# A two-layer encoder on one core: a Mamba scan with one decay block a head, and down projections that begin with two units in one pass

## The chip, the cores and the metric

The kernel runs on one core of a Trainium2 chip. The metric is the device time of one execution in microseconds (us). The median of three runs of the kernel before is 2797.76 us (2797.67 to 2798.13).

## The reference

Batch 1, 256 tokens, width 2048, two layers, all in float32. Layer 0 is a gated short convolution mixer and an MLP, layer 1 a bidirectional Mamba-2 mixer (64 heads of 64 channels in 8 groups, state 128, chunks of 128 tokens) and an MLP of the same form; each of the four sublayers has an adaLN modulation of its own from the condition vector.

```
for each sublayer:  shift, scale, gate = split(silu(c) @ ada_w + ada_b)
                    h = rms_norm(x, g) * (1 + scale) + shift
                    x = x + gate * sublayer(h)
MLP:    square(relu(h @ w1)) @ w2                       (2048 -> 8192 -> 2048)
conv:   b, c, v = split(h @ w_in);  (b * dwconv3(c * v)) @ w_out
Mamba:  z, x, B, C, dt_raw = split(h @ w_in); x, B, C = silu(dwconv3(.) + bias)
        dt = softplus(dt_raw + dt_bias), one forward and one backward for each head
        per direction: cum = running sum of dt * a;  y[t] = sum over s of
              (C[t] . B[s]) * exp(cum[t] - cum[s]) * dt[s] * x[s],   s <= t (backward: s >= t)
        y = y_fwd + y_bwd + d * x;  u = group_rms_norm(y * silu(z)) * g;  u @ w_out
```

## The kernel before, in words

Activations lie as channels x tokens (16 blocks of 128 channels, 256 tokens). Each float32 product is made of three: the weights are split into a high half `wh` (fp32r) and a rest `wl`, the activations into a high and a low part that lie side by side in `hcat` (input of a layer) or `hid` (between its two products). One **unit** makes 128 output channels: two halves of weights, 16 blocks of the contraction, for each block one matmul of `wh` against 512 columns and one of `wl` against 256 (L918, L921), into one of the two PSUM banks `psm`. For a unit `v`, in each engine's order:

- SP loads the raw weights of half after half (512 KB, four buffers) and, where the schedule has one, a 1 MB tile of modulation weights into `adat` (two buffers).
- ACT (`step`, `unit`) makes the high half of half 2v+4 (L674), copies bank v to `ta` (L679), and makes the high half 2v+5.
- DVE (`step`) makes the low half 2v+4 (L1121), adds the two parts of the bank into `tt` or `pad` (L1153, L1200, L1279), makes the low half 2v+5, does what the unit needs besides, and reduces a modulation tile where there is one (L1134).
- POOL makes low parts of activations (L558, L592) and adds to the residual `x` (L548).

A unit of PE waits until unit v-2 has been added (`at_least(pe, summed, u - 1)`), since it shares that unit's bank. `pair` (L928 on) is a second form: two units at once, block by block, into both banks; it waits for `summed` of u, that is also for the unit just before it. Before, it is used for the first units behind each norm, for the dt projection and for the first two output units of the Mamba mixer (`src == "chunk 0"`). All other down projections (`gated`) start with single units, whose first one waits block by block for the blocks of `hid` that its predecessor, an up projection or conv unit, is still making.

The order is written out in `walk`: conv (24 pairs of triples), its output (16 units), MLP 0 in four quarters of 16 up and 16 down units, dt, groups 0 to 4, the first output units of the Mamba mixer (over the channels of groups 0 to 3), groups 5 to 7, the late output slabs (`late_outs`, half a unit each), MLP 1 in four quarters.

A **group** of the Mamba mixer is ten units, called slots 0 to 9: B, C, four blocks of x, four of z. The scan of group g-1 runs between the units of group g, that of group 7 between the late slabs. Its steps by slot, before:

- Slot 0: PE makes the scores (L1014) and transposes x to tokens (L1020). ACT copies two blocks of scores (L793, L794) and the transposed x (L798). POOL multiplies x by the dt of each direction, from `dgrp` (two operations of 1024 columns, L582). DVE masks the scores into `gcat` (L1333).
- The running sums lie in DRAM; SP loads them, broadcast, into `em[1..4]` (four pieces of two heads each). `em[1]` lies in `normt`, `em[2]` and `em[3]` in `dec`, `em[4]` in the second buffer of `adat`, which is why SP holds modulation tiles back there (`resume`).
- `segments` (DVE, L1375, four operations of 128 columns) and `decays` (ACT, L785, four exponentials of 256 columns) for pieces 1 to 4; piece 1's segments come at the end of the group before, the other pieces' in slots 0 to 2, the decays in slots 0 to 3.
- `masked` in slots 1 to 4 (DVE, L1303, L1305, L1309): products of decays and scores into 3 x 128 columns for each direction.
- Slots 3 to 6: PE makes two heads each (L1034), for each head three products for either block of tokens, so 12 in a slot. A float32 product shows as two records.
- Slot 6: ACT copies y out of PSUM (L802). Slot 7: PE transposes it back (L1043), DVE adds the skip term and multiplies by z (L1318, L1323). Slots 8 and 9: the group norm (L805, L586, L1050, L808, L1340, L1344), then the high and low parts for the output product (L818, L592).
- `columns_of` (DVE, L1354, L1357), at the end of each group: the group's 8 columns of dt and sums are copied out of `dtS` and `ncS`, and the gaps between blocks made.

`dt_late` makes dt and the sums in group 0; `DT_ALL` is the count of its DVE steps after which the sums may be used.

In a slot DVE's order is `scan_piece`, low half, `scan_mid` (here `masked`), silu of the unit before, addition, low half, taps, `scan_late` (here `segments`); ACT's is `scan_piece`, high half, copy, high half, centre tap, tanh, `scan_late` (here `decays`).

## Time and profile before

| | before |
|---|---|
| median of 3 runs | 2797.76 us |
| profiled execution | 2797.92 us |
| its span (first to last instruction) | 2796.2 us |
| mean granted TensorE clock | 0.982 |
| PE busy | 2601.4 us, 93% |
| DVE busy | 2140.2 us, 77% |
| ACT busy | 1354.1 us, 48% |
| POOL busy | 781.6 us, 28% |
| read from HBM | 675.58 MB, 242 GB/s over the span |

Busy shares are means over stages that differ. The Mamba part lies between 1236 and 2050 us, the conv layer and MLP 0 ahead of it, MLP 1 behind it. A row of the waits says which engine and instruction waited for which; a row of the timeline has its start, its duration (of all merged instructions, if x is over 1), and in brackets the idle time ahead of it with what ended it. Matmuls overlap, so durations of several don't add up: the distance from start to start is what counts.

### The profile page before, as it was taken

The page shows a single profiled execution, that of the slowest core. Times are in us where ns is not written, and L with a number is a line of the kernel's source. Part 1 is how long each engine was busy: PE and PEld are TensorE (multiplying, and loading weights), DVE is VectorE, ACT ScalarE, POOL GpSimd, SP SyncE. Part 2 cuts the span into 40 slices and gives each one's busy share as a digit, 9 for nine tenths or more (in the row PEclk, how much of TensorE's full clock was granted, in tenths as well). Part 3 has the DMA queues.
Part 4 walks back from the last instruction along what each step waited for, and adds up shares of the span by engine and source line. Part 5 has one row for each costly group of instructions (what it writes and reads, how often), then busy time and mean ns, then how long its engine had stood idle before and what let it go on. Part 6 is the DMA issues. An engine that isn't in the chain of part 4 may idle for free. (4 is left out here: it accounts for less than half of the span.)

```text
span 2796.2 us, 45031 instructions
## 1 busy us (share of the span) xinstructions
PE 2601.4 (93%) x14956; PEld 2269.0 (81%) x14956; DVE 2140.2 (77%) x2597; ACT 1354.1 (48%) x2038; POOL 781.6 (28%) x714
## 2 busy tenths in 40 slices
PE   0399999999999999999999899999989999999998
PEld 0288888888888888878888788888878888888887
DVE  6988889886978879986777787778799555555554
ACT  2244444544444444465555544556454444444454
POOL 3522225442434434530111031111345111111123
PEclk9899999999999999999999999999999999999999
DMA  8888889686878879945554485555559555555554
GB/s 331 306 321 318 316 330 363 239 315 229 331 287 314 316 280 324 358 168 196 166 166 166 158 311 207 167 166 165 204 215 338 192 188 188 188 188 188 189 188 142
DMA packets 171670, 679.62 MB, mean 243 GB/s; under 512 B 18672, under 2 KB 35312, under 8 KB 146704
## 3 DMA queue, kind: packets, MB, share of 16 engines
q1 hardware_dynamic: 171488, 677.75, 68.6%
q8 instruction: 79, 1.29, 0.2%
q14 instruction: 55, 0.45, 0.0%
q0 software_dynamic: 48, 0.13, 0.0%
HBM read 675.58 MB, written 2.23 MB: 242 GB/s over the span
## 5 line engine op out<-in xcount | busy, mean ns | idle before, releaser
L1121 DVE TENSOR_TENSOR wl<-raw,wh 128x1024 fp32r<-128x1024 f32 x862 | 1130.0, 1311 | 461.6 <-ACT wh L674 459.7
L918 PE MATMUL psm<-hcat,wh 128*128 128x512 f32 x3984 | 1270.0, 400 | 16.0 <-DVE pad L1279 10.8
L674 ACT ACTIVATE wh<-raw 128x1024 fp32r<-128x1024 f32 x866 | 911.0, 1052 | 215.8 <-PE psm L921 141.4
L921 PEld LDWEIGHTS psm<-hcat,wl 128*128 128x128 f32 x3984 | 755.4, 190 | 179.6
L918 PE MATMUL psm<-hid,wh 128*128 128x512 f32 x2528 | 797.7, 397 | 10.2 <-POOL hid L558 5.7
L921 PE MATMUL psm<-hcat,wl 128*128 128x256 f32 x3984 | 788.7, 280 | 0.0
L918 PEld LDWEIGHTS psm<-hcat,wh 128*128 128x128 f32 x3984 | 613.7, 191 | 19.3 <-issue 13.2
L921 PEld LDWEIGHTS psm<-hid,wl 128*128 128x128 f32 x2528 | 476.4, 188 | 112.5
L921 PE MATMUL psm<-hid,wl 128*128 128x256 f32 x2528 | 497.7, 278 | 0.0
L1134 DVE CUSTOM_DVE_ANT_0 adat<-adat,cond 128x2048 f32<-128x2048 f32 x176 | 427.0, 2426 | 21.1 <-DMA adat<-in_ada 13.8
L918 PEld LDWEIGHTS psm<-hid,wh 128*128 128x128 f32 x2528 | 386.4, 189 | 12.0 <-POOL hid L558 7.0
L558 POOL TENSOR_TENSOR hid<-tt,hid 128x256 f32 (+1 forms) x128 | 176.3, 1377 | 481.5 <-ACT hid L742 481.5
L548 POOL TENSOR_TENSOR x<-x,tt 128x256 f32 (+1 forms) x154 | 198.5, 1289 | 400.7 <-DVE tt L1200 400.7
L510 POOL COPY modc<-modt 128x1 f32 (+1 forms) x192 | 175.4, 919 | 233.4 <-DVE modt L1134 233.4
L679 ACT ACTIVATE ta<-psm 128x256 f32<-128x256 f32 x257 | 96.7, 376 | 182.9 <-PE psm L921 176.7
L742 ACT ACTIVATE hid<-tt 128x256 f32 (+1 forms) x128 | 53.5, 418 | 266.4 <-DVE tt L1222 266.4
L679 ACT ACTIVATE ta<-psm,mods 128x256 f32<-128x256 f32 x160 | 75.5, 472 | 215.3 <-PE psm L921 209.8
L1200 DVE SCALAR_TENSOR_TENSOR tt<-psm,mods,ta 128x256 f32<-128x256 f32 x160 | 76.6, 479 | 108.5 <-ACT ta L679 108.3
L586 POOL TENSOR_TENSOR zs<-zs 128x512 f32<-128x512 f32 x8 | 10.4, 1294 | 402.0 <-ACT zs L805 402.0
L940 PE MATMUL psm<-hcat,wh 128*128 128x512 f32 x128 | 49.1, 469 | 78.5 <-POOL wl L656 55.8
L683 ACT ACTIVATE normt<-x 128x256 f32<-128x256 f32 (+1 forms) x80 | 33.3, 417 | 141.8 <-POOL x L548 100.1
L1153 DVE TENSOR_TENSOR tt<-ta,psm 128x256 f32<-128x256 f32 x177 | 73.1, 413 | 23.6 <-ACT ta L679 23.6
(174 smaller groups left out, 1684.7 us busy)
## 6 DMA issues: line engine op xcount, KB each, us to landing
raw<-in_w SPq DMA_DIRECT2D x866, 512.0 KB, 4.2
adat<-in_ada SPq DMA_DIRECT2D x176, 1024.0 KB, 6.4
xs<-in_ada SPq DMA_DIRECT2D x8, 1024.0 KB, 6.7
zs<-in_ada SPq DMA_DIRECT2D x8, 1024.0 KB, 6.2
dec<-running_sums SPq DMA_DIRECT2D x32, 256.0 KB, 5.3
normt<-running_sums SPq DMA_DIRECT2D x16, 256.0 KB, 4.7
adat<-running_sums SPq DMA_DIRECT2D x16, 256.0 KB, 5.3
x<-in_xT SPq DMA_DIRECT2D x1, 2048.0 KB, 17.1
```

Source lines behind the costliest of these rows:

```text
L510: pool.tensor_copy(modc[:, bass.ds(a.v, 1)], modt[:, a % 2:a % 2 + 1]).then_inc(mod_copied, 1)
L548: pool.tensor_tensor(x[:, nn.v, :], x[:, nn.v, :], tt[:, v % 2, :], ALU.add).then_inc(stored, 1)
L558: pool.tensor_tensor(hid[:, jj.v, T:2 * T], tt[:, v % 2, :], hid[:, jj.v, 0:T].bitcast(F32), ALU.subtract).then_inc(stored, 1)
L674: act.activation(wh[:, h % 4, :], raw[:, h % 4, :], ACT.Copy).then_inc(hi_done, 1)
L679: act.activation(ta[:, v % 2, :], psm[v % 2][:, 0:T], ACT.Copy, scale=scale).then_inc(copied, 1)
L742: act.activation(hid[:, jj.v, 0:T], tt[:, v % 2, :], ACT.Copy).then_inc(relu_hi, 1)
L918: pe.matmul(bank[:, :], wh[:, h % 4, (k + i) * P:(k + i + 1) * P], src[:, kb + i, :], start=(kb + i == 0), stop=(kb + i == KB - 1), skip_g ...
L921: mm = pe.matmul(bank[:, T:2 * T], wl[:, h % 4, (k + i) * P:(k + i + 1) * P], src[:, kb + i, 0:T], start=False, stop=(kb + i == KB - 1), s ...
L1121: dve.tensor_tensor(wl[:, h % 4, :], raw[:, h % 4, :], wh[:, h % 4, :].bitcast(F32), ALU.subtract).then_inc(lo_done, 1)
L1134: dve.tensor_tensor_reduce(t, t, cond[:, :], 1.0, 0.0, ALU.mult, ALU.add, modt[:, a % 2:a % 2 + 1]).then_inc(ada_done, 1)
L1153: return dve.tensor_tensor(tt[:, v % 2, :], ta[:, v % 2, :], psm[v % 2][:, T:2 * T], ALU.add)
L1200: return dve.scalar_tensor_tensor(out=tt[:, v % 2, :], in0=psm[v % 2][:, T:2 * T], scalar=gcol, in1=ta[:, v % 2, :], op0=ALU.mult, op1=ALU ...
```

## The change

The scan: one decay block per head and per block of tokens. Inside a block both directions go into one 128 x 128 matrix (the dt of each direction is multiplied in on ACT and DVE, in `decays` and `masked`), so that a head needs two products instead of six. What crosses from one block of tokens to the other is made by two products 128 x 512 for all eight heads of a group, from x weighted by `far_in` (POOL), into `psr[1]` and `psr[0]`, and scaled by `far_out` when y is gathered, which DVE now does in place of ACT's copy. The columns `far_in`, `far_out` and the gaps are made once for all heads in `dt_late`, and `columns_of` is gone. The buffers of pieces 1 and 4 move (`hv`, a third `dec`), so that modulation tiles are no longer held back.

The down projections: `gated` on PE begins with `pair` wherever its first unit follows a change of source, in nine more places (the conv's output, four quarters of MLP 0, four of MLP 1).

```diff
-DT_AV, DT_TOK, DT_CUM, DT_ALL = 11, 13, 14, 15
+DT_AV, DT_TOK, DT_CUM, DT_FAR, DT_ALL = 11, 13, 15, 22, 24
...
-        em = [None, normt[:, :].rearrange("p (k t) -> p k t", k=4), dec[:, 0], dec[:, 1]]
-        em.append(adat[:, 1, 0:6 * T].rearrange("p (k t) -> p k t", k=4))
+        em = [None, hv, dec[:, 0], dec[:, 1], dec[:, 2]]
+        columns = normt[:, 4 * T:6 * T].rearrange("p (n d h) -> p n d h", n=4, d=2)
+        far_in, far_out, gapS, midS = (columns[:, i] for i in range(4))
...
@@ SP, load_sums @@
                 at_least(sp, y_head, g * HG + HG)
-                if piece == 4:
-                    at_least(sp, ada_done, ADA_LATE if g.c >= GA - 1 else ADA_OUT0)
...
@@ POOL, scan_piece, slot 0 @@
                     at_least(pool, xt_copied, g * 2 + 2)
-                    at_least(pool, grp_in, g * 2 + 2)
-                    for d in (1, 0):
-                        if d == 0:
-                            at_least(pool, xd_ready, g * 2 + 1)
-                        src, dst = (xd[:, i, :, :].rearrange("p c (h e) -> p c h e", e=HD) for i in (0, d))
-                        pool.tensor_tensor(dst, src, dgrp[:, :, d, :].unsqueeze(3).to_broadcast([P, 2, HG, HD]),
+                    pool.wait_ge(dt_dve, DT_ALL)
+                    for d in range(2):
+                        src, dst = (xd[:, i, d, :].rearrange("p (h e) -> p h e", e=HD) for i in (0, 1))
+                        pool.tensor_tensor(dst, src, far_in[:, d, heads(g)].unsqueeze(2).to_broadcast([P, HG, HD]),
                                            ALU.mult).then_inc(xd_ready, 1)
...
@@ ACT @@
+            def dt_far():
+                act.wait_ge(dt_dve, DT_FAR)
+                act.activation(far_in, far_in, ACT.Exp).then_inc(dt_act, 1)
+                act.activation(far_out, far_out, ACT.Exp, scale=-1.0).then_inc(dt_act, 1)
...
             def decays(g, piece):
                 at_least(act, seg_done, g * 4 + piece)
-                for d in range(2):
+                act.wait_ge(dt_dve, DT_ALL)
+                at_least(act, g_ready, g * 4 + 4)
+                for c in range(2):
+                    here = slice(c * P, (c + 1) * P)
                     for i in range(2):
-                        row, h = em[piece][:, 2 * d + i, 0:T], 2 * (piece - 1) + i
-                        ins = act.activation(row, row, ACT.Exp, bias=ngrp[:, d, d, h:h + 1])
+                        own, other = em[piece][:, 2 * c + i, here], em[piece][:, 2 * (1 - c) + i, here]
+                        h = g.c * HG + 2 * (piece - 1) + i
+                        act.activation(own, own, ACT.Exp, bias=ncS[:, c, c, h:h + 1])
+                        ins = act.activation(other, lower[c], ACT.Copy, scale=dtS[:, c, 1, h:h + 1])
...
-                if s == 6:
-                    at_least(act, y_head, g * HG + 2 * HG)
-                    for ch in range(2):
-                        act.activation(ytok[:, ch, :], psy[ch][:, :], ACT.Copy).then_inc(y_tok, 1)
...
@@ PE, gated @@
-                both = first and src == "chunk 0"
-                if both:
+                if first:
                     pair(u, ready, hid)
-                for s in range(2 if both else 0, 4):
-                    unit(u + s, hid, ready if first and s == 0 else None)
+                for s in range(2 if first else 0, 4):
+                    unit(u + s, hid)
...
@@ PE, scan_piece @@
                 if 3 <= s <= 6:
+                    if s == 3:
+                        at_least(pe, g_copied, g * 2 + 2)
+                        at_least(pe, g_ready, g * 4 + 4)
+                        at_least(pe, xd_ready, g * 2 + 2)
+                        pe.matmul(psr[1][:, :], gf[:, P:T], xd[:, 1, 0, :], start=True, stop=True, skip_group_check=True)
+                        pe.matmul(psr[0][:, :], gb[:, 0:P], xd[:, 1, 1, :], start=True, stop=True, skip_group_check=True)
                     for h in (2 * (s - 3), 2 * (s - 3) + 1):
...
-                        for ch, terms in ((0, ((mf, 0, 0, 0), (mb, 2 * P, 1, 0), (mb, 0, 1, 1))),
-                                          (1, ((mf, P, 0, 0), (mf, 2 * P, 0, 1), (mb, P, 1, 1)))):
-                            for i, (m, at, d, sc) in enumerate(terms):
-                                mm = pe.matmul(psy[ch][:, cols], m[:, at:at + P], xd[:, d, sc, cols],
-                                               start=(i == 0), stop=(i == 2), skip_group_check=True)
+                        for ch in range(2):
+                            mm = pe.matmul(psy[ch][:, cols], em[s - 2][:, 2 * ch + h % 2, ch * P:(ch + 1) * P],
+                                           xd[:, 0, ch, cols], start=True, stop=True, skip_group_check=True)
...
@@ DVE, dt_late, slot 9 @@
+                    dve.wait_ge(dt_dve, DT_CUM + 1)
+                    for d in range(2):
+                        own(dve.tensor_tensor(gapS[:, d, :], ncS[:, d, 1 - d, :], ncS[:, d, d, :], ALU.subtract))
+                        own(dve.tensor_tensor(far_in[:, d, :], ncS[:, d, d, :], midS[:, d, :], ALU.add))
+                        own(dve.tensor_tensor(far_out[:, d, :], ncS[:, 1 - d, d, :], midS[:, d, :], ALU.add))
+                    dve.wait_ge(dt_act, 6)
+                    for d in range(2):
+                        own(dve.tensor_tensor(far_in[:, d, :], far_in[:, d, :], dtS[:, d, d, :], ALU.mult))
...
@@ DVE, masked @@
-                dve.tensor_tensor(e[:, 0:2, T:3 * P], e[:, 2:4, P:T],
-                                  gf[:, T:3 * P].unsqueeze(1).to_broadcast([P, 2, P]), ALU.mult)
-                dve.tensor_tensor(e[:, 2:4, T:3 * P], e[:, 0:2, 0:P],
-                                  gb[:, T:3 * P].unsqueeze(1).to_broadcast([P, 2, P]), ALU.mult).then_inc(far_done, 1)
-                at_least(dve, far_done, g * 4 + piece)
-                e4 = e[:, :, 0:T].rearrange("p (d i) t -> p d i t", d=2)
-                dve.tensor_tensor(e4, e4, gcat[:, :, 0:T].unsqueeze(2).to_broadcast([P, 2, 2, T]), ALU.mult)\
-                    .then_inc(em_ready, 1)
+                for c in range(2):
+                    for i in range(2):
+                        h = g.c * HG + 2 * (piece - 1) + i
+                        other = e[:, 2 * (1 - c) + i, c * P:(c + 1) * P]
+                        ins = dve.scalar_tensor_tensor(out=other, in0=upper[c], scalar=dtS[:, c, 0, h:h + 1], in1=other,
+                                                       op0=ALU.mult, op1=ALU.add)
+                ins.then_inc(sel_done, 1)
+                at_least(dve, sel_done, g * 4 + piece)
+                for c in range(2):
+                    own, other = (e[:, 2 * k:2 * k + 2, c * P:(c + 1) * P] for k in (c, 1 - c))
+                    ins = dve.tensor_tensor(own, own, other, ALU.mult)
+                ins.then_inc(em_ready, 1)
...
@@ DVE, scan_piece, ahead of the slot's low half @@
+                if s == 6:
+                    at_least(dve, y_head, g * HG + 2 * HG)
+                    for ch in range(2):
+                        dve.tensor_tensor(ytok[:, ch, :].rearrange("p (h e) -> p h e", e=HD),
+                                          psr[ch][:, :].rearrange("p (h e) -> p h e", e=HD),
+                                          far_out[:, 1 - ch, heads(g)].unsqueeze(2).to_broadcast([P, HG, HD]),
+                                          ALU.mult).then_inc(y_far, 1)
+                    at_least(dve, y_far, g * 2 + 2)
+                    for ch in range(2):
+                        dve.tensor_tensor(ytok[:, ch, :], ytok[:, ch, :], psy[ch][:, :], ALU.add).then_inc(y_tok, 1)
...
-            def columns_of(g):
...
@@ DVE, group @@
                 silu(g, u + (GU - 1), GU - 1)
-                columns_of(g)
                 segments(g, 1)
```

## Rows read from the trace of the kernel before

**Rows 1.** The waits of PE from 1236 to 2050 us: total, times, longest.

```profile
PE psm L918 <- DVE pad L1279: 10.8, 6, 1.9
...
PE psr L1082 <- issue: 4.6, 1, 4.6
```

**Rows 2.** Windows: length, busy of PE, PEld, DVE, ACT, POOL, PEclk, DMA share, GB/s.

```profile
500.00:1216.00 716.00, 713.26 (x4080) 621.17 (x4079) 601.63 (x622) 340.31 (x476) 295.82 (x227) 1.00 0.82 300
...
2162.00:2165.30 3.30, 3.24 (x10) 2.76 (x11) 1.84 (x4) 2.39 (x3) 0.14 (x2) 0.51 0.09 35
```

**Rows 3.** The timeline of DVE in slots 0 and 1 of a group: start, duration.

```profile
1460.82 0.42 DVE L1279 TENSOR_TENSOR pad<-ta,psm 128x256 f32<-128x256 f32 x1
...
1462.30 0.48 DVE L1285 SCALAR_TENSOR_TENSOR acc<-pad,parg,acc 128x256 f32<-128x256 f32 x1
...
1466.32 1.23 DVE L1121 TENSOR_TENSOR wl<-raw,wh 128x1024 fp32r<-128x1024 f32 x1 [1.98 <-ACT wh L674]
1467.46 0.42 DVE L1303 TENSOR_TENSOR normt<-normt,gcat 128x256 f32<-128x256 f32 x1
...
1469.39 0.42 DVE L1392 SCALAR_TENSOR_TENSOR bT<-th,acc 128x256 f32<-128x256 f32 x1
1469.73 0.41 DVE L1279 TENSOR_TENSOR pad<-ta,psm 128x256 f32<-128x256 f32 x1
```

**Rows 4.** The timeline of ACT in the same slots.

```profile
1463.65 1.69 ACT L785 ACTIVATE normt<-normt,ngrp 128x256 f32<-128x256 f32 x4
1465.25 1.04 ACT L674 ACTIVATE wh<-raw 128x1024 fp32r<-128x1024 f32 x1
```

**Rows 5.** The timeline of PE: the first two heads, the transposes of slot 7.

```profile
1469.62 2.87 PE L1034 MATMUL psy<-xd,normt 128*128 128x64 f32 x24 [0.86 <-DVE normt L1309]
...
1505.75 1.09 PE L1043 MATMUL psr<-ident,xd 128*128 128x128 f32 x8 [0.98 <-ACT xd L802]
```

**Rows 6.** Groups by line and shape: busy us, mean ns of one, idle before.

```profile
L1014 PE MATMUL psr<-cT,bT 128*128 128x256 f32 x32 | 8.2, 379 | 0.0
...
L793 ACT ACTIVATE gcat<-psr 128x128 f32<-128x128 f32 x8 | 2.1, 258 | 0.0
```

**Rows 7.** The timeline of POOL and DVE at the end of a group.

```profile
1451.75 2.44 POOL L592 TENSOR_TENSOR hid<-xs,hid 128x1024 fp32r<-128x1024 f32 x1 [12.48 <-ACT hid L818]
...
1454.30 3.89 POOL L582 TENSOR_TENSOR xd<-xd,dgrp 128x1024 f32<-128x1024 f32 x2
...
1529.59 2.44 POOL L592 TENSOR_TENSOR hid<-xs,hid 128x1024 fp32r<-128x1024 f32 x1 [12.49 <-ACT hid L818]
...
1451.95 2.42 DVE L1357 TENSOR_TENSOR gap<-ngrp 128x8 f32<-128x8 f32 x2
1454.48 4.38 DVE L1375 SCALAR_TENSOR_TENSOR normt<-normt,gap 128x128 f32<-128x128 f32 x4
```

**Rows 8.** The timeline of DVE at the end of group 0.

```profile
1301.92 1.14 DVE L1375 SCALAR_TENSOR_TENSOR normt<-normt,gap 128x128 f32<-128x128 f32 x4 [4.92 <-DMA normt<-running_sums]
```

**Rows 9.** The timeline of PE and DVE where down projections begin, and behind the existing pass.

```profile
2336.87 0.63 PE L918 MATMUL psm<-hid,wh 128*128 128x512 f32 x2
...
2337.60 0.42 DVE L1153 TENSOR_TENSOR tt<-ta,psm 128x256 f32<-128x256 f32 x1 [0.30 <-ACT ta L679]
...
948.88 0.63 PE L918 MATMUL psm<-hid,wh 128*128 128x512 f32 x2
...
950.57 0.41 DVE L1153 TENSOR_TENSOR tt<-ta,psm 128x256 f32<-128x256 f32 x1
...
2152.19 0.68 PE L918 MATMUL psm<-hid,wh 128*128 128x512 f32 x2
...
2157.35 0.41 DVE L1153 TENSOR_TENSOR tt<-ta,psm 128x256 f32<-128x256 f32 x1
...
2162.06 0.80 PE L918 MATMUL psm<-hid,wh 128*128 128x512 f32 x1 [4.54 <-POOL hid L558]
...
1619.91 0.47 PE L918 MATMUL psm<-hid,wh 128*128 128x512 f32 x1 [1.17 <-DVE tt L1200]
```

More of the change, by code:

```diff
@@ L135, in first_unit, with heads @@
     return g * GU + U_GA
+def heads(g):
+    return slice(g.c * HG, g.c * HG + HG)
 def blocks(g):
@@ L203, in build @@
         ncS = sb("ncS", [P, 2, 2, HEADS])
-        dec = sb("dec", [P, 2, 4, 3 * P])
+        dec = sb("dec", [P, 3, 4, T])
         bT = sb("bT", [P, T])
@@ L388, in load_half, with load_ada @@
                 sp.dma_start(raw[:, h % 4, :], w[h.v]).then_inc(raw_in[h % 4], 16)
-            def load_ada(a, resumed=False):
-                if not a.terms and (a.c >= ADA or a.c - ADA_OUT0 in (0, 1) and not resumed
-                                    or a.c - ADA_LATE in (0, 1) and not resumed):
+            def load_ada(a):
+                if not a.terms and a.c >= ADA:
                     return
@@ L473, in norm @@
                 sp.wait_ge(out_done, 64)
-            def resume(a, g):
-                at_least(sp, y_head, g * HG)
-                for k in range(2):
-                    load_ada(a + k, True)
             walk(sp, lambda u, j, ada_at, a, f: steps(u, 6, ada_at, a),
@@ L484, in _ @@
                  lambda: steps(At(U_DT), 1, (), None),
-                 group, late_outs, norm, resume=resume)
+                 group, late_outs, norm)
         @block.gpsimd
@@ L827, in group @@
                         dt_log()
+                    elif s == 9:
+                        dt_far()
             def late_outs(a):
@@ L996, in dt_late @@
                                   start=False, stop=False, skip_group_check=True)
-                        mm = pe.matmul(psr[2][rows, far * P:(far + 1) * P], avS[:, far, rows], up[:, :],
-                                       start=False, stop=True, skip_group_check=True)
+                        pe.matmul(psr[2][rows, far * P:(far + 1) * P], avS[:, far, rows], up[:, :],
+                                  start=False, stop=True, skip_group_check=True)
+                    for near, rows in ((0, f), (1, b)):
+                        mm = pe.matmul(psr[3][:, rows], ones[:, :], avS[:, near, rows], start=True, stop=True,
+                                       skip_group_check=True)
                     mm.then_inc(dt_pe, 1)
@@ L1268, in dt_late @@
                     own(dve.tensor_copy(hv[:, 0, :], psr[2][:, 0:T]))
+                    own(dve.tensor_copy(midS.rearrange("p d h -> p (d h)"), psr[3][:, 0:P]))
                 if s == 9:
@@ L1367, in segments @@
                 at_least(dve, cb_in[s - 1], g * 32 + 32)
[L1368 to L1369 removed]
+                dve.wait_ge(dt_dve, DT_ALL)
                 for c in range(2):
@@ L1372, in segments @@
                     for i in range(2):
-                        h = 2 * (s - 1) + i
+                        h = g.c * HG + 2 * (s - 1) + i
                         own, other = em[s][:, 2 * c + i, here], em[s][:, 2 * (1 - c) + i, here]
-                        ins = dve.scalar_tensor_tensor(out=own, in0=other, scalar=gap[:, c, h:h + 1], in1=own,
+                        ins = dve.scalar_tensor_tensor(out=own, in0=other, scalar=gapS[:, c, h:h + 1], in1=own,
                                                        op0=ALU.add, op1=ALU.min)
```

29 lines of the change are left out of this document (4 added, 25 removed).

## The prediction

> **What bounds the kernel now.** First read who TensorE (PE) waits for. A projection, conv or MLP unit is 32 matmuls, at 716 us for 4080 of them (127.5 units) 5.6 us, and nearly everywhere the next follows at once [rows 2]. Between 1236 and 2050 us (the Mamba part) the wait that comes again in the groups is for the DVE addition that empties a unit's bank, six times and 10.8 us [rows 1]. So less PE work pays only where others are not later still, and the second look goes to what DVE and ACT do in a group.
>
> In a slot of a group (one unit) DVE runs, in this order: a low half, `masked`, a silu, the addition into `pad`, a low half, two taps, `segments`. ACT runs tanh, `decays`, a high half. These lean on each other in a ring: addition to first tap 1.48 us, first tap to `decays` (over tanh) 1.35, `decays` to high half 1.60, high half to DVE's low half 1.07, low half to `masked` 1.14, `masked` to silu 1.93, silu to addition 0.34 [rows 3, 4]. That is 8.91 us, just the distance of the two additions, 1460.82 and 1469.73 [rows 3]. Four such turns follow each other in a group (slots 0 to 4), 35.6 us. In those slots PE needs the unit and two heads (24 records in 2.87 us, 0.11 each beside the tail), 8.4 us, and waits for `masked` ahead of them [rows 5]. **The ring is slower than PE already.** The other slots are PE's. POOL's first step of a group comes again after 77.84 us [rows 7].
>
> **The scan, step by step.**
> (a) PE: 24 records become 8 for two heads, 16 x 0.11 = 1.76 us less in each of four slots, 7.0 a group. Two products 512 wide come; one 256 wide is 8.2/16 = 0.51 us [rows 6], so about 0.9 each, 1.8 a group. Net 5.2 us a group on PE, but in slots where it waits. What counts is the ring.
> (b) ACT: `decays` issues 8 instructions of 128 columns for 4 of 256. Bounds for one: 0.40 us (1.60/4, width costing nothing), and 0.155, a plain 128-wide copy's 0.258 less the 0.1 by which neighbours overlap (a `decays` instruction among four, 1.69 in all, overlaps so too) [rows 4, 6]. They read bias or scale from a column as the 0.40 ones do, and half the width should save about 0.11, so I take 0.29: 2.3 us, +0.7 a turn, between -0.4 and +1.6.
> (c) DVE `masked`: four 128-wide instructions with a column scalar, like `segments` (1.14 for four [rows 8]), then two of 256 elements at 0.34 (silu to addition [rows 3]): 1.82 for 1.93, -0.1. A turn becomes 9.5 us, four +2.4; by the bounds -1.9 to +6.0.
> (d) `columns_of` goes, and POOL multiplies 2x512 columns instead of 2x1024. Now DVE's two tiny subtractions take 2.42 us while POOL makes a low part of 2.44, and four `segments` instructions take 4.38 (elsewhere 1.14) and end at 1458.86, 0.67 after POOL's 3.89 us of products [rows 7, 8]. The products halve, so DVE is free 1.9 to 2.5 us earlier; I take 2.1.
> The Trainium skill, SBUF — State Buffer, section "SBUF: two separate sides", says that a DVE operation with two SBUF inputs and a GpSimd operation that reads SBUF exclude each other for a whole instruction, and the later one blocks. By that rule, the trace agrees; if they shared bandwidth instead, the dropped subtractions would count in full and the sum would be some 5 us lower.
> (e) y leaves PSUM by DVE instead of ACT, in four operations of 512 columns. The 256-wide addition issues in 0.34, the 1024-wide low half in 1.14 [rows 3], so 0.60 each, with 0.25 for the dependence and the tail 2.65 us. DVE comes to it after slot 5's taps: from the fourth turn's addition A a turn without `decays` and `masked` is 5.4, low half and taps 2.5, so A+7.9, done A+10.55. PE starts the transposes at 1505.75, which is A+9.3 (A is 1460.82+35.62), after a wait of 0.98 for ACT's copy [rows 5]. So +1.25 us, and all of slots 7 to 9 stands behind it. ACT wins its copies' time back and has no use for it.
> In five groups the first addition waits for POOL: -2.1 + 2.4 + 1.25 = +1.5 each, 7.5 us. In two (the first scanned, and the first behind the output units) PE's own queue was as late, and nothing is won at (d): +3.5 each, 7 us.
> (f) The decay columns are made once, at the end of group 0: six small subtractions or additions, two exponentials, two products, ahead of the count for which SP waits before it issues the loads of sums. DVE waits 4.92 us for their landing already [rows 8]. It all moves back by 2.2 us (ten at 0.15 to 0.2, a crossing to ACT and back). SP's raw loads queue behind; four buffers cover them.
> (g) Group 7 is scanned among the late output slabs, where PE waits 4.6 us once [rows 1]. (d) takes 2.1 of that; four head slots lose 1.76 each less 1.8 for the wide products, but a slab then waits for a DVE sum behind the slower ring. I take 7 us less (2 to 9).
> (h) PE will idle about 4 us before the transposes (its unit ends at A+6.3, y is there at A+10.55), and 2 to 3 us before heads. After a wait of 4.54 us for `hid` [rows 9] the granted clock was 0.51 over the next 3.3 us [rows 2], the 1.2 GHz level, so 1.65 us of work was lost. Before slot 7 this counts in full, in slots 1 to 5 the slack covers it. Some 0.7 us a group: 5 (0 to 12).
> (i) The loads of modulation tiles are no longer held back for the scan's buffer, and the copies of columns go. Nothing waits for either but (d); 0.
> Scan: 7.5 + 7 + 2.2 + 5 - 7 = +15 us.
>
> **The down projections.** Nine places (the conv's output, four quarters of each MLP) now begin with two units in one pass. It needs both banks, so PE must wait until the last up unit is copied by ACT and added by DVE, where now the first down unit starts at once. In three quarters of the last MLP it starts as at 2336.87, and the addition ends at 2338.02 [rows 9]: 1.17 us new, three times 3.5. In three of the first MLP's, behind a slow low half, as from 948.88 to 950.98 [rows 9]: 2.1, three times 6.3. By the same reading 3.5 at its first quarter, 4.4 at the conv's output, and at the last MLP's first quarter, where DVE is behind with modulation tiles, 2152.19 to 2157.76 [rows 9], 5.6. Sum 23.3 us. Behind the pass the next unit waits for copy and addition again, as behind the one existing pass over `hid`: 1.17 us idle [rows 9], 1.34 start to start above the usual step, nine times 12.1. What goes: the pass comes to the last block 5 us later, so the present waits for it vanish, 4.7 (idle 4.54 [rows 9]), 3.5 and 1.3 in three places, 9.5 us. The other six wait for no block now. Net 23.3 + 12.1 - 9.5 = +25.9. Half clock after the longer waits 3 us (0 to 8). DVE idles in the pass and has two units' additions and tiles behind it, 2 us (0 to 5). **+31 us.** A free bank would cover the entry, and there is none.
>
> **Sum.** 15 + 31 = +46 on the profiled execution's 2797.92 us (span 2796.2 and 1.7 around it; the median of the runs is 2797.76, the same): 2844 us.
>
> **Rivals.**
> 1. The ring shrinks below PE. If `decays` ran in ACT's idle time, off the ring, a turn would be 7.3 us, four 29.2 for 35.6; with (d) and (e) -7.3 a group, -51 in seven: 2797.9 + 31 - 51 - 7 = 2771, faster. It decides where a turn falls below 7.9 us (28 turns must return 45 us). For it: ACT has idle time in each turn. Against: its program has `decays` behind tanh and ahead of the high half that DVE waits for. 7%.
> 2. The entries of the passes cost nothing, because DVE comes to the addition sooner than now: 2844 - 23 - 3 = 2818. Against: nothing ahead of the boundary changes. 6%.
> 3. ACT's narrow instructions cost 0.155: -1.9 - 2.1 + 1.25 = -2.7 in five groups, -0.6 in two, +2.2, -7 to -9, no half clock: scan -20, 2797.9 + 26 to 31 - 20, 2804 to 2809. 9%; the lower half of it is within reach of no change.
> 4. Half clock throughout: each head slot with 2 to 3 us of idle runs at 1.2 GHz, a unit takes up to 11 us for 5.6, and PE leads again by some 2 us in each of 28 slots: 2844 - 5 + 56 = 2895. Against: waits of 1.9 us [rows 1] leave the slots behind them mostly at full clock. 3%. The Trainium skill, TensorE: Matmul & The Clock Gate, section "HAM oscillation — how this bites in real kernels", has such a case, a kernel whose idle gaps between bursts bring the lower clock back each time.
> My case as summed: 75%.
>
> **Numbers.** 2844 us. Range 2809 to 2867: the low end is (b) near its lower bound, the high end (b) at 0.40 (+3.6 in seven groups, 25, less 2 for slack). A difference of 0.2% (5.6 us) is about what a measurement of this kernel can tell from none. Faster 0.09, within 0.04, slower 0.87.
>
> **What would show it.** In the profile after: additions into `pad` 9.5 us apart in slots 0 to 4 (above 9 supports (b), below 8.5 refutes it); PE gaps before heads of 2 to 3 us and before the transposes of about 4, both ended by DVE; nine passes with a wait for a DVE `tt` ahead (1.2, 2.1, or 3.5 to 5.6 us) and one of 1.2 behind; no wait for `hid` left; a middle group's period near 80 us. I am wrong if that is below 76, or if PE enters the passes without a wait.

## The result, and the profile after

| | before | after |
|---|---|---|
| median | 2797.95 us | 2887.43 us |
| lowest and highest of 4 runs | 2797.67 to 2800.89 | 2886.08 to 2888.44 |
| span of the profiled execution | 2796.2 us | 2885.3 us |
| mean granted TensorE clock | 0.982 | 0.970 |

Ratio 1.0317, 95% interval 1.0299 to 1.0335: slower by 89.5 us, where 46 were forecast, and above the range. The direction was right; the size was not, so the question is what the other 43 us are.

First the waits of TensorE in the profile after, 1290 to 2126 us, the Mamba part as in [rows 1] (columns: who waited for whom, us in total, times, the longest):

```profile
engine line waited for: us in total, times, longest us
PE psy L1035 <- DVE dec L1323: 42.5, 18, 2.8
PE psr L1044 <- DVE xd L1361: 40.3, 8, 6.5
PE psy L1035 <- DVE normt L1323: 8.2, 7, 1.3
```

The wait for `pad`, first in [rows 1], is gone. Two others have come: for the masked decays ahead of the heads (2.8 us and less), which the prediction named, and for y ahead of the transposes: 40.3 us in 8, up to 6.5, where "about 4" stood. Next the additions into `pad` and `masked` ahead of them on DVE, after (start, duration, instruction), to hold against [rows 3]:

```profile
1505.07 0.42 DVE L1289 TENSOR_TENSOR pad<-ta,psm 128x256 f32<-128x256 f32 x1
...
1512.47 1.13 DVE L1317 SCALAR_TENSOR_TENSOR normt<-gcat,dtS,normt 128x128 f32<-128x128 f32 x4
1513.63 0.76 DVE L1323 TENSOR_TENSOR normt<-normt 128x256 f32<-128x256 f32 x2
...
1514.65 0.41 DVE L1289 TENSOR_TENSOR pad<-ta,psm 128x256 f32<-128x256 f32 x1
...
1524.21 0.41 DVE L1289 TENSOR_TENSOR pad<-ta,psm 128x256 f32<-128x256 f32 x1
...
1533.76 0.41 DVE L1289 TENSOR_TENSOR pad<-ta,psm 128x256 f32<-128x256 f32 x1
```

They are 9.56 us apart, forecast 9.5. But the group has a period of 83.2 us, where the forecast had "near 80" (77.8 before). On ACT the eight exponentials and copies of `decays` stand 0.29 us apart (three of them):

```profile
1507.90 0.39 ACT L785 ACTIVATE normt<-normt,ncS 128x128 f32<-128x128 f32 x1
1508.20 0.39 ACT L786 ACTIVATE normt<-gcat,dtS 128x128 f32<-128x128 f32 x1
1508.49 0.39 ACT L785 ACTIVATE normt<-normt,ncS 128x128 f32<-128x128 f32 x1
```

So the ring did what was said, and the loss lies behind it. Then the end of the scan of the same group, DVE:

```profile
1550.16 0.48 DVE L1295 SCALAR_TENSOR_TENSOR acc<-pad,parg,acc 128x256 f32<-128x256 f32 x1
1550.68 0.48 DVE L1298 SCALAR_TENSOR_TENSOR acc<-pad,parg,acc 128x256 f32<-128x256 f32 x1
1552.59 1.23 DVE L1122 TENSOR_TENSOR wl<-raw,wh 128x1024 fp32r<-128x1024 f32 x1 [1.43 <-ACT wh L665]
1553.74 1.28 DVE L1355 TENSOR_TENSOR xd<-psr,normt 128x512 f32<-128x512 f32 x2
1555.05 1.28 DVE L1361 TENSOR_TENSOR xd<-xd,psy 128x512 f32<-128x512 f32 x2
```

y (L1355, L1361; `ytok` lies in `xd`) doesn't follow the taps (L1298), as the prediction has it, but the low half behind them (L1122), which waits 1.43 us for ACT's high half. TensorE then:

```profile
1556.39 1.97 PE L1044 MATMUL psr<-ident,xd 128*128 128x128 f32 x8 [6.54 <-DVE xd L1361]
1558.01 1.20 PE L917 MATMUL psm<-hcat,wh 128*128 128x512 f32 x2
```

With the fourth turn's addition A at 1543.32, that is A+13.1 for a forecast of A+10.55. And eight transposes take 1.97 us for 1.09 [rows 5], the two products behind them 1.20 for 0.62: half clock. The first MLP's first pass has it as well, the last MLP's second has not (rows of the windows: stretch, length, busy time of PE, PEld, DVE, ACT, POOL, granted clock, DMA share, GB/s):

```profile
599.40:602.80 3.40, 3.34 (x12) 2.89 (x13) 1.51 (x3) 0.42 (x1) 0.73 (x1) 0.59 1.03 372
...
2417.30:2428.70 11.40, 11.35 (x64) 9.79 (x64) 2.79 (x3) 1.89 (x3) 0.74 (x1) 1.00 0.43 138
1556.40:1559.70 3.30, 3.30 (x14) 3.06 (x15) 3.04 (x7) 0.42 (x1) 0.00 (x0) 0.58 0.20 30
```

The granted clock 0.59 over a stretch that ends at full speed is the 1.2 GHz level. That pass was entered after 3.35 us of idleness, the one at full clock after 1.12, and both are left after 1.58 to 1.60:

```profile
599.46 0.72 PE L939 MATMUL psm<-hid,wh 128*128 128x512 f32 x2 [3.35 <-DVE wl L1122]
...
614.00 0.70 PE L917 MATMUL psm<-hid,wh 128*128 128x512 f32 x2 [1.58 <-DVE tt L1201]
```

```profile
2417.35 0.72 PE L939 MATMUL psm<-hid,wh 128*128 128x512 f32 x2 [1.12 <-DVE tt L1154]
...
2428.36 0.40 PE L943 MATMUL psm<-hid,wl 128*128 128x256 f32 x2
2430.36 0.73 PE L917 MATMUL psm<-hid,wh 128*128 128x512 f32 x2 [1.60 <-DVE tt L1201]
```

**Where the time went.** Both executions have the same products of weights in nearly the same order, and the starts of the same ones cut both into stages. A down projection is counted from the last product ahead of it to its own last one. What each stage takes more than before, in us, for the profiled execution of the changed kernel and of experiments below ("first": the first group that scans; "behind out": the group behind the output units; "rest": start, norms, group 0, output units). Where a kernel has no edit, such a sum can still differ by 3 us: before_decays_early changes nothing in the down projections.

| | down projections (9) | first | behind out | other 5 groups | late slabs | rest | all |
|---|---|---|---|---|---|---|---|
| predicted | 31 | 6.4 | 4.2 | 11.0 | -7 | 0 | 46 |
| predicted, less its half clock | 28 | 5.7 | 3.5 | 7.5 | -7 | 0 | 38 |
| **after** | 42.2 | 9.6 | 7.5 | 30.0 | -3.0 | 2.9 | 89.2 |
| scan_alone | 0.3 | 9.5 | 7.5 | 30.2 | -3.0 | 1.7 | 46.2 |
| pass_alone | 42.5 | -0.2 | 0.0 | 0.2 | -0.6 | 1.9 | 43.8 |
| y_ahead | 40.7 | 7.6 | 4.7 | 19.9 | -7.0 | 1.5 | 67.5 |
| warm_pass | 31.6 | 10.3 | 7.8 | 30.7 | -3.0 | 3.2 | 80.7 |
| warm_y | 40.8 | 7.9 | 5.1 | 20.6 | -4.6 | 2.5 | 72.4 |
| y_ahead_warm | 31.6 | 6.9 | 2.4 | 9.4 | -7.0 | 3.8 | 47.2 |
| decays_early | 40.5 | 1.9 | 0.0 | -9.2 | -4.5 | 3.2 | 31.9 |
| before_decays_early | 3.1 | -4.8 | -3.6 | -21.9 | -0.3 | -2.2 | -29.7 |
| best_no_pass | 0.8 | 0.1 | -3.8 | -22.4 | -6.9 | -0.2 | -32.4 |
| best_y_warm | 1.4 | -3.7 | -6.6 | -38.3 | -6.3 | 1.1 | -52.3 |

### The profile page after: what moved, and what is told of

It is laid out like the page before. It is cut to its first block and busy times, and to the rows that moved or that the text cites. A ratio compares the mean times of both kernels' runs of the same rounds, so it can differ in the third digit from the quotient of the medians.

```text
span 2885.3 us, 44320 instructions
## 1 busy us (share of the span) xinstructions
PE 2595.8 (90%) x14480; PEld 2244.3 (78%) x14480; DVE 2149.6 (75%) x2702; ACT 1366.6 (47%) x2152; POOL 770.0 (27%) x714
## 5 line engine op out<-in xcount | busy, mean ns | idle before, releaser
L1122 DVE TENSOR_TENSOR wl<-raw,wh 128x1024 fp32r<-128x1024 f32 x862 | 1135.3, 1318 | 512.9 <-ACT wh L665 510.8
L917 PE MATMUL psm<-hid,wh 128*128 128x512 f32 x2240 | 706.6, 397 | 15.2 <-DVE tt L1201 15.0
L917 PEld LDWEIGHTS psm<-hcat,wh 128*128 128x128 f32 x3984 | 620.1, 193 | 10.1 <-DVE wl L1122 6.5
L920 PEld LDWEIGHTS psm<-hid,wl 128*128 128x128 f32 x2240 | 420.8, 188 | 99.4
L920 PE MATMUL psm<-hid,wl 128*128 128x256 f32 x2240 | 440.3, 278 | 0.0
L917 PEld LDWEIGHTS psm<-hid,wh 128*128 128x128 f32 x2240 | 340.9, 189 | 19.0 <-issue 10.0
L939 PE MATMUL psm<-hid,wh 128*128 128x512 f32 x320 | 110.4, 429 | 26.3 <-DVE wl L1122 16.2
L577 POOL TENSOR_TENSOR zs<-zs 128x512 f32<-128x512 f32 x8 | 10.4, 1303 | 453.5 <-ACT zs L802 453.5
```

Of the source, the lines that this page charges most:

```text
L917: pe.matmul(bank[:, :], wh[:, h % 4, (k + i) * P:(k + i + 1) * P], src[:, kb + i, :], start=(kb + i == 0), stop=(kb + i == KB - 1), skip_g ...
L920: mm = pe.matmul(bank[:, T:2 * T], wl[:, h % 4, (k + i) * P:(k + i + 1) * P], src[:, kb + i, 0:T], start=False, stop=(kb + i == KB - 1), s ...
L939: pe.matmul(bank[:, :], wh[:, h % 4, k * P:(k + 1) * P], src[:, kb, :], start=(kb == 0), stop=(kb == KB - 1), skip_group_check=True)
L1122: dve.tensor_tensor(wl[:, h % 4, :], raw[:, h % 4, :], wh[:, h % 4, :].bitcast(F32), ALU.subtract).then_inc(lo_done, 1)
```

## The experiments

Twelve kernels ran. Eleven have the median of four or five executions, with the kernel before timed beside them (2798.2 to 2799.0 us); peel_all has a single execution. "Less" is the difference to the changed kernel's 2887.4, where nothing else is said.

**scan_alone and pass_alone.** The change in its two parts. The first has the change without the new passes, the second the new passes alone:

```diff
 # PE, gated
-                if first:
+                both = first and src == "chunk 0"
+                if both:
                     pair(u, ready, hid)
-                for s in range(2 if first else 0, 4):
-                    unit(u + s, hid)
+                for s in range(2 if both else 0, 4):
+                    unit(u + s, hid, ready if first and s == 0 else None)
```

> The kernel after with the down projections begun by single units again, so the scan's edit alone. Theory: the two parts add up, and the scan carries +44 to +48 us (47 us more in the eight stretches that hold a group's scan, 3 less in the late slabs): 2840 to 2846 us. A group of the middle keeps its period of 83 to 84 us. Rival: the two parts lean on each other (half clock or DVE's backlog carried over from the passes), then the scan alone is below +35 us.

> The kernel before with its down projections begun by two units in one pass in the nine places, so this edit alone. Theory: +40 to +44 us, 2838 to 2842 us, with 3.3 us in each quarter of the last MLP and 5.7 in the first MLP's. My prediction had +31. Rival: the passes alone cost the predicted 31 us, and the rest comes from the scan's edit (buffers moved, modulation tiles loaded sooner).

Measured 2844.38 us (ratio 1.0163, interval 1.0146 to 1.0180) and 2843.26 (1.0161, 1.0144 to 1.0178), +46 and +45. The second is 1.3 us above what was expected. They add up to the change's 89.5 within 2 us, and the stages of either are those of the whole: the parts hardly touch each other. Both are dearer than forecast, the scan by 31 us, the passes by 14.

**y_ahead.** Is it the place of y? The four DVE operations go from `scan_mid` (behind the low half) to `scan_piece` (ahead of it):

```diff
             def scan_piece(g, s):
                 par2 = g % 2
+                if s == 6:
+                    at_least(dve, y_head, g * HG + 2 * HG)
...
+                        dve.tensor_tensor(ytok[:, ch, :], ytok[:, ch, :], psy[ch][:, :], ALU.add).then_inc(y_tok, 1)
                 if s == 7:
```

> The kernel after with DVE's gathering of y moved ahead of slot 6's low half, which is where my prediction had it; in the change it stands behind that low half, which waits for ACT. Theory: PE's wait before the transposes falls by 2.6 us in each of seven groups and the half clock behind it partly goes: 18 to 26 us less than the kernel after, 2861 to 2869 us. Rival: the low half is then late by the 2.6 us of the gathering and PE waits for it instead, 0 to 5 us less.

Measured 2862.86 us (1.0230, 1.0213 to 1.0247): 24.6 less. The wait ahead of the transposes is now 3.87 us in all seven groups:

```profile
1547.96 1.97 PE L1044 MATMUL psr<-ident,xd 128*128 128x128 f32 x8 [3.87 <-DVE xd L1337]
```

With A at 1537.55 that is A+10.4, for the forecast's A+10.55. The late slabs win the 7 us that (g) gave them. The stages give 21.7 us, not 24.6, because the profiled execution was 2.5 us slower than the median: 14.9 in the groups, 4.0 in the late slabs.

**decays_early.** Is it the ring that sets the slots? `decays` is issued behind ACT's second high half of the slot instead of ahead of the first one:

```diff
 # ACT, unit
                 copy(v, 1.0 if conv_unit else 0.5)
                 hi(v * 2 + 5)
+                if early:
+                    early()
 # ACT, group
+                    early = (lambda s=s: decays(g - 1, s + 1)) if scanning and s <= 3 else None
+                    unit(g, u + s, s, scanning, early)
-                    unit(g, u + s, s, scanning)
-                    if scanning:
+                    if scanning and s > 3:
                         scan_late(g - 1, s)
```

> The kernel after with the decays of slots 0 to 3 issued by ACT before the centre tap, in the time in which it waits for DVE's addition, instead of behind tanh (in the groups; the late slabs are left). Theory (a ring of DVE and ACT sets slots 0 to 4): a turn falls from 9.56 by the 2.3 us of decays to 7.2 to 7.6, and with four turns in seven groups 50 to 65 us go: 2822 to 2837 us. Rival (PE sets these slots, through its half clock): additions stay 9 us and more apart or PE fills the time, less than 15 us go.

Measured 2830.24 us (1.0115, 1.0098 to 1.0132), 57 less. The additions:

```profile
1503.16 0.41 DVE L1294 TENSOR_TENSOR pad<-ta,psm 128x256 f32<-128x256 f32 x1
...
1507.06 1.23 DVE L1127 TENSOR_TENSOR wl<-raw,wh 128x1024 fp32r<-128x1024 f32 x1 [0.39 <-ACT wh L665]
...
1510.38 0.41 DVE L1294 TENSOR_TENSOR pad<-ta,psm 128x256 f32<-128x256 f32 x1
```

7.22 us apart, where rival 1 had 7.3. Four turns are 9.4 us shorter; a group is 7.5 to 7.8 shorter, since TensorE's waits for y grow from 40.3 us to 47.5.

**before_decays_early.** The same move in the kernel before.

> The kernel before with only its decays moved behind ACT's high half. Ours: a turn's ring falls from 8.91 to 7.3 us there as well, below TensorE's own 8.4 us with 24 records a head pair, so four turns return 4 x 0.5 = 2 us a group, 14 in seven, and somewhat more where the first addition is late: 2775 to 2786 us. So the move is worth less there than in the changed kernel (57 us), because TensorE is the next bound. Rival, the move is worth the same in both: 2741 us. Rival, TensorE was the bound all along: 2796 to 2799.

Measured 2768.84 us (0.9895, 0.9879 to 0.9912), 29.6 less: twice what I expected, half of the other. TensorE is the next bound, as said: its heads come 8.27 us after each other. But a middle group gains 4.2 to 4.7 us, not 2. In the one that starts at 1370 us slot 2 gives 1.1, each of slots 3 to 5 0.6, and slot 6 1.2, where TensorE's wait for y ahead of the transposes, 0.98 us before [rows 5], is gone.

The trace also shows what I had not seen: the kernel before has half clock in six of its seven groups that scan. In four it follows the 1.9 us wait for `pad` [rows 1] (behind the one that ends at 1461.39 the granted clock is 0.61 over 3.3 us), in two a wait of 2.1 or 2.4 us for `masked`. With `decays` early it is left in three groups. It explains little of the gain: two groups with as much of it as before (1.7 us of work lost) gain 4.2 us, two that lose all 3.4 us of it gain 4.6 and 4.7.

**warm_pass and warm_y.** Is the longer work behind an idle stretch half clock, and what does it cost? TensorE multiplies the identity into an idle bank ahead of the wait; each such product takes 0.23 to 0.25 us. (Both kernels already do so ahead of the sums of three norms, in `keep_warm`.)

```diff
-            def pair(u, ready, src=hcat):
+            def pair(u, ready, src=hcat, warm=0):
+                for _ in range(warm):
+                    pe.matmul(psy[1][:, 0:P], ident[:, :], ident[:, :], start=True, stop=True,
+                              skip_group_check=True)
+                    warm = (16, 7, 0, 20 if isinstance(src, At) and src.c == U_MLP1 and not src.terms else 0)[layer]
+                    pair(u, ready, hid, warm)
-                    pair(u, ready, hid)
 # PE, scan_piece, warm_y
                 if s == 7:
+                    if warm:
+                        for _ in range(18):
+                            pe.matmul(psr[3][:, 0:P], ident[:, :], ident[:, :], start=True, stop=True,
+                                      skip_group_check=True)
                     at_least(pe, y_tok, g * 2 + 4)
```

> The changed kernel with products of the identity into an unused bank (16, 7 and 20 of them, about 0.23 us each) on TensorE ahead of the waits of six passes: the conv's output, the first MLP's four, the last MLP's first. If the 1.5 us (2.1 at the last MLP's first) by which these passes are longer than the other three (12.97 for 11.4 us) is the half clock after the idle entry, they end 1.2 to 1.8 us earlier each: 2877 to 2881 us. If the longer passes are something else (waits for weights or blocks inside), 2886 to 2889.

> The changed kernel with 18 such products (4.2 us) on TensorE ahead of its wait for y in slot 7 of seven groups. The transposes (1.97 us for 8) and the first blocks of the unit behind them run at half clock after 5.0 to 6.5 us of idleness. If that costs in full, as slot 7 is TensorE's, 1.0 to 1.7 us a group come back: 2876 to 2881 us. If the half clock there is covered by a later wait: 2885 to 2888.

Measured 2878.24 us (1.0284, 1.0267 to 1.0302), 9.2 less, and 2870.98 (1.0260, 1.0243 to 1.0277), 16.5 less. In warm_y:

```profile
1545.52 4.18 PE L1041 MATMUL psr<-ident 128*128 128x128 f32 x36
1552.20 1.09 PE L1048 MATMUL psr<-ident,xd 128*128 128x128 f32 x8 [2.51 <-DVE xd L1365]
1553.05 0.71 PE L917 MATMUL psm<-hcat,wh 128*128 128x512 f32 x2
```

```profile
1552.20:1555.50 3.30, 3.29 (x22) 2.99 (x23) 3.30 (x7) 0.42 (x1) 0.00 (x0) 1.00 0.19 55
```

22 records in the 3.3 us behind the wait, for 14 above, and clock 1.00 after 2.51 us of idleness. In warm_pass the first pass of the first MLP takes 11.4 us for 12.97. So longer useless work made the kernel faster, and by more than I had put even on a whole scan's half clock.

**y_ahead_warm.** Both corrections at once, with 12 products ahead of the transposes.

> The changed kernel with the two steps that the prediction had wrong put right: y gathered ahead of slot 6's low half, as the prediction placed it, and products of the identity on TensorE ahead of the long waits (12 ahead of the transposes of y in seven groups, 16, 7 and 20 ahead of six passes). In y_ahead units 7 and 8 of a group and the transposes take 2.7 us more than at full clock (13.19 for 11.40, 1.97 for 1.09); the passes gave 9.2 us back. If placement and half clock are all that the prediction had wrong, a group's period is 2 to 2.5 us above the kernel before's (+1.5 predicted, and 0.5 of rest), and the time is 2862.9 - 7 x 2.3 (1.6 to 2.7) - 9.2 = 2835 to 2843 us; the prediction's own sum without its 8 us of half clock is 2836. If a third cause is in the scan, above 2848.

Measured 2843.72 us (1.0161, 1.0148 to 1.0175), 0.7 above the upper edge of what was expected. By stages nothing large is left in the scan: the five middle groups cost 9.4 us (forecast 7.5), the two others 9.3 (9.2), the late slabs -7.0 (-7), the down projections 31.6 (28). 3.8 us lie in the rest, 2.2 of it in the norm behind the first MLP, where I had put no cost; I have not followed them. That the total is the forecast's 2844 is chance: the forecast held 8 us of half clock ahead of slot 7 and in the passes, which the identity products take out here, and the rest and the passes' exits come in their place. Half clock itself is not gone: the mean granted clock is 0.980, y_ahead's 0.976. None is left in the new passes and in slots 7 to 9; in the head slots TensorE's waits cover it.

**peel_all.** From a pass's last product to the next unit it is 1.46 us from start to start where the code behind is written out (the last quarter of the first MLP), and 1.85 to 1.88 in the other eight of nine, where ACT and DVE are in an innermost loop. The first body of each loop was written out on every engine, not on TensorE alone:

```diff
-            def bodies(n, f, peel=lead):
+            def bodies(n, f, peel=True):
```

> The changed kernel with the first body of every loop written out on ACT, DVE, POOL and SP too, as it is on TensorE, so that in the conv's output and at the last MLP's first quarter the first four down units have no value of a loop's register in their waits and addresses. If it is these values that make ACT's copy and DVE's addition behind a pass start 0.25 us later each (0.69 and 0.77 us after what they wait for, where the passes in straight-line code have 0.43 and 0.51), the step from the pass's last product to the next unit falls there from 1.86 to about 1.46 us, and stays 1.88 in the quarters that lie in an outer loop. If it is something else (the pass's place, the transfers), it stays 1.86. The time changes by a few us at most, 2880 to 2888.

A single execution, 2882.01 us. At the conv's output and the last MLP's first quarter the step fell to 1.46, as expected, and so it did in two more places outside an outer loop. But in the four quarters inside one it fell as well, from 1.88 to 1.54:

```profile
2424.57 0.39 PE L943 MATMUL psm<-hid,wl 128*128 128x256 f32 x2
2426.23 0.74 PE L917 MATMUL psm<-hid,wh 128*128 128x512 f32 x2 [1.27 <-DVE tt L1201]
```

There the outer loop's register is still in the waits and addresses. So it is not a register as such that costs 0.4 us, but being in the innermost loop's body; whether through its own register or the instructions around it stays open.

**best_no_pass, best_y_split, best_y_warm.** What the changed scan is worth when its ring and y are put right: no new passes, decays early, and y ahead (first kernel); y's two products by the far decays already behind slot 4's taps, into the half of `xd` that is free by then (second); 8 identity products ahead of the transposes (third).

```diff
-        ytok = xd[:, 0]
+        ytok = xd[:, 1]
             def scan_piece(g, s):
+                if s == 5:
+                    at_least(dve, y_head, g * HG + HG + 4)
+                    for ch in range(2):
+                        dve.tensor_tensor(ytok[:, ch, :].rearrange("p (h e) -> p h e", e=HD),
...
+                if s == 6:
+                    at_least(dve, y_head, g * HG + 2 * HG)
+                    at_least(dve, y_far, g * 2 + 2)
```

> The changed scan with its decays behind ACT's high half, y gathered ahead of the slot's low half, and no pass at the down projections (but the one that was there). Ours: of the +89.5 us of the change the passes are +43 to +45, the decays in the ring 57, and y's place 25 or somewhat more (with the decays out of the ring, TensorE waits 5.9 us a group ahead of the transposes, all for y). The sum is 2887.4 - 44 - 57 - 25 to 35 = 2751 to 2762 us, below the kernel before. Rival, the gains overlap (what one returns the other would have returned too, since both stand ahead of slot 7): 2775 to 2790.

> best_no_pass with y gathered in two steps: the two products by the far decays (1.28 us) behind slot 4's taps, where DVE is idle for 1.43 us before slot 5's low half, and only the two additions behind slot 5's taps; y lies in the half of its buffer that the wide products have read. Ours: y is there 1.2 us earlier in each of seven groups, TensorE's wait of 3.8 us ahead of the transposes becomes 2.6, and nothing else moves: 2767.3 - 8.5 = 2759 us, down to 2750 if the clock recovers with the shorter wait. Rival, the products land in the ring of the turns (the idle time is not there in most groups): 2766 to 2770 us.

> best_y_split with 8 products of the identity (1.9 us) on TensorE ahead of its wait for y in slot 7. The same edit in the changed kernel (18 of them) returned 16.4 us in seven groups, 2.3 a group. Ours: 1.2 to 2.3 us a group here too, 8 to 16 us below best_y_split: 2736 to 2751 us, below both kernels. Rival, with 2.6 us of wait the clock stays up anyway: the same as best_y_split within 2 us.

Measured 2767.29 us (0.9889, 0.9872 to 0.9905), 2752.52 (0.9835, 0.9820 to 0.9850) and 2745.58 (0.9812, 0.9799 to 0.9826). The first lies between its two cases: the gains overlap, but by less than the rival had. The second is within what was expected. The third is 6.9 us below the second, where 8 to 16 were expected. With y split, DVE's operations fill the idle time and the low half waits 0.24 us for ACT instead of 1.43 (rows of best_y_warm):

```profile
1480.63 0.48 DVE L1308 SCALAR_TENSOR_TENSOR acc<-pad,parg,acc 128x256 f32<-128x256 f32 x1
1481.03 1.28 DVE L1341 TENSOR_TENSOR xd<-psr,normt 128x512 f32<-128x512 f32 x2
1482.55 1.23 DVE L1132 TENSOR_TENSOR wl<-raw,wh 128x1024 fp32r<-128x1024 f32 x1 [0.24 <-ACT wh L665]
```

best_y_warm beats both kernels, the one before by 53 us. With only its decays moved, the old scan gains 30, the changed one (best_no_pass, y put right as well) 31, the same within 2 us; the rest comes from the split and the clock. No run gives the old scan identity products or other help of that kind, so which scan is better at its best is not shown.

## Why the prediction was wrong, and where it was right

**(b), (c), the ring: right.** A turn is 9.56 us for 9.5, `decays` 0.29 us apart as taken. The Trainium skill, ScalarE: Activation LUTs, section "What ACT_TABLE_LOAD costs", gives 280 ns and 0.833 ns a column for an instruction with a column as bias, and an overlap of 93 ns between neighbours; an estimate from that is 0.387 us long and 0.294 apart at 128 columns, and the trace agrees (0.39, 0.29). The range I kept for it, up to 0.40, could have been closed. Rival 1 had the turn right too: off the ring it is 7.22 us for 7.3. It had the group wrong: with y where the forecast put it (best_no_pass) the seven groups return 26.1 us for its 51. Half clock behind the wait for y, which it had at nothing, takes 1.5 to 2.8 us of a group (transposes 0.9, the unit behind them 0.6 to 1.9), and (d) wins nothing in two groups; the rest I have not followed. They return 48.6 only with y split and identity products (best_y_warm). It was no rival to this change, whose code leaves `decays` in the ring. Rival 3 falls with the 0.29 us, and rival 2 with the entries of the passes (below).

**(d): right.** From the scores to the first addition 14.38 us before, 12.10 after, in the group of the rows: 2.3 for 2.1. POOL's two products take 2.19 us for 3.89 [rows 7].

**(e), y by DVE: the step that failed.** It said "from the fourth turn's addition A a turn without `decays` and `masked` is 5.4, low half and taps 2.5, so A+7.9, done A+10.55". The durations hold (2.6 us for the four operations, and A+10.4 in y_ahead). The place does not. I had read the change's lines as standing in DVE's `scan_piece`, and the heading of that hunk in the diff above ("scan_piece, ahead of the slot's low half") says so too, wrongly: they stand in `scan_mid`, behind the low half. The operations therefore queue behind an instruction that waits 1.43 us for ACT and then runs 1.15, and come 2.55 us later. With y in its forecast place (y_ahead) the median falls by 24.6 us. By stages 14.9 of it are in the seven groups, less than 7 x 2.55 = 18, since the unit behind the transposes loses more to half clock there (7.2 to 7.5 us from start to start, for 6.2 to 7.3), and 4.0 in the late slabs (where I had -7 and the trace has -3.0).

**(h), half clock in the scan: right mechanism, too small.** I put 0.7 us a group, 5 in all. warm_y returned 13.5 in the groups, and y_ahead_warm is 13.5 below y_ahead, 1.9 a group: transposes 0.9, units 7 and 8 up to 1.8. One wait for `hid` of the kernel before, with 1.65 us lost over 3.3 us [rows 2, 9], was my only row for it. The trace before had more. Its existing pass over `hid`, whose exit I read, runs at half clock at its start:

```profile
1606.05 0.77 PE L940 MATMUL psm<-hid,wh 128*128 128x512 f32 x1 [3.77 <-issue]
```

```profile
1606.05:1609.35 3.30, 3.30 (x11) 2.82 (x12) 3.27 (x5) 1.30 (x2) 1.93 (x1) 0.57 0.35 108
```

It takes 12.69 us, and passes at full clock 11.4. The argument against rival 4, that waits of 1.9 us leave the slots behind them mostly at full clock, was a misreading as well: of five such waits in the groups four are followed by half clock. Rival 4 (half clock throughout, 2895) still comes near the measured time for another reason. In the changed kernel 11 of 28 head slots have some half clock (granted clock 0.68 to 0.77 over the unit), but the turns stay 9.56 us, so the slack covers it, as the prediction said.

The Trainium skill, TensorE: Matmul & The Clock Gate, section "HAM oscillation — how this bites in real kernels", names a kernel whose idle gaps bring the lower clock back. The trace agrees in kind: clock 0.58 behind 6.54 us of idleness, 1.00 behind 2.51 in warm_y.

**The down projections: right by wait, two terms short.** The entries are as read: 1.12 us in the last MLP for 1.17, 2.1 in the first, and no wait for a block of `hid` is left. With the clock kept up the nine places cost 31.6 us, for 28 without half clock. (1) "1.34 start to start above the usual step" came from the one pass with written-out code behind it; in loops it is 1.75, eight times 0.4, 3.3 us. (2) Half clock was put at 3 us; six passes have it behind entries of 2.0 to 5.5 us, 1.55 us in four of them and 2.1 in two, and warm_pass returned 10.6 in these stages. Together with the 28 that is 41.9 of the 42.2.

**(f), (g): right in size.** Without y's misplacement the first scanned group costs 6.9 us (5.7 with (f)) and the late slabs -7.0. (i) was put at nothing, and no run tests it by itself.

In short, by the stages: 46 forecast, 19 for the place of y, 16 for clock beyond the 8 forecast (13.5 and 10.6 returned in the groups and the passes), 3 for the loops' exits. That is 84 of 89; 2 us more in the groups and 3 in the rest are not explained.

## What to carry to other kernels

- For an operation that moves to another engine, find the instruction directly ahead of it in that engine's program, and what that one waits for; the duration was the easy half here, the queue place cost 19 us by the stages and 25 by the medians.
- A ring of three engines sets the pace of a slot when TensorE has room: moving one helper (`decays`) out of it was worth 57 us in one kernel and 30 in the other.
- An idle stretch of TensorE can be paid twice, by its length and by the work behind it at 1.2 GHz. Where the wait can't go, a few products of no use ahead of it, no longer than the wait, gave back 7 to 16 us. The clock can't be read off a wait of TensorE alone, so look at the granted clock behind several waits of the same kind.

## What the runs showed of the hardware that was not expected

- Idleness of 2.1 us ahead of a pass was followed by a stretch at half clock that lost 1.55 us; 1.12 us, and 2.51 us behind 4.2 us of identity products, were not. The length of the wait alone doesn't decide it: of the first MLP's passes, entered alike, one in peel_all (11.42 us) and one in pass_alone (11.38) ran at full clock, and in decays_early even the first, behind 3.35 us of idleness:

```profile
599.49 0.70 PE L944 MATMUL psm<-hid,wh 128*128 128x512 f32 x2 [3.35 <-DVE wl L1127]
```

```profile
599.49:610.88 11.39, 11.39 (x64) 9.77 (x64) 2.67 (x4) 1.48 (x2) 0.74 (x1) 1.00 0.67 252
```

- Behind a pass ACT's copy and DVE's addition come some 0.25 us later each in the body of an innermost loop than in code written out; leaving such a pass takes 0.4 us longer.
- The kernel before runs at half clock too in six of its seven scanned groups, in four of them behind the 1.9 us wait for `pad` [rows 1], at a cost of 1.7 or 3.4 us of work; a fifth such wait was not followed by it. Moving `decays` left 1.7 us in three groups and none in the others, but the time gained hardly depends on it.
